# Two transformer-like blocks on one core: a unit's products with the low half of the weights move behind all those with the high half

## The reference, cut to what matters

```python
def first_block(x, mem, ...):
    z = _rmsnorm(x, g_mix) @ w_in                 # 1024 x 11272: three branches, their gates
    kv = _rmsnorm(mem, g_mem) @ w_mem_kv          # cross attention's keys and values
    ...                                           # stick-breaking attention, mLSTM, cross attention
    x = x + (g0 * (y_sb @ w_sb_proj) + g1 * (y_ml @ w_ml_proj) + g2 * (y_x @ w_x_proj)) @ w_out
    x = x + square(relu(_rmsnorm(x, g_mlp) @ w_ff1)) @ w_ff2

def second_block(x, ...):
    proj = rmsnorm(x, norm_mix_pre_w) @ w_in      # dilated attention and a Mamba-2 mixer, their gates
    ...
    h = x + rmsnorm((g_att * att + g_ssm * ssm) @ w_out, norm_mix_post_w)
    f = square(relu(rmsnorm(h, norm_ffn_pre_w) @ w_up)) @ w_down
    return h + rmsnorm(f, norm_ffn_post_w)
```

## Time and profile before

| | |
|---|---|
| median of 3 runs | 1284.5 us |
| the profiled execution's own time | 1283.23 us |
| its span (first to last instruction) | 1281.1 us |
| TensorE matmul (PE) busy | 1234.9 us, 96% |
| TensorE weight load (PEld) busy | 1209.5 us, 94% |
| VectorE (DVE) busy | 799.1 us, 62% |
| ScalarE (ACT) busy | 659.4 us, 51% |
| L236 matmuls | 8976 in 188 units |
| DMA, mean | 164 GB/s |

### The profile page before, as it was taken

The page is one execution under the profiler, slowest core; times in us unless marked ns, Lnnn a source line. Parts: engine busy times, 40 slices in busy tenths (PEclk is TensorE's granted clock), DMA queues, the critical chain, the costliest instruction groups (busy, mean ns, idle before and its releaser), DMA issues. The chain is left out here.

```text
span 1281.1 us, 22409 instructions
## 1 busy us (share of the span) xinstructions
PE 1234.9 (96%) x9900; PEld 1209.5 (94%) x9900; DVE 799.1 (62%) x866; ACT 659.4 (51%) x764; POOL 10.5 (1%) x23
## 2 busy tenths in 40 slices
PE   7999999999999999999989999899899998999996
PEld 6999999999999999999989989898899997999996
DVE  6655666777664557774456567787874554777442
ACT  6443444677543445553344468777864444455330
POOL 0000000000000000000000000000000000000000
PEclk9999999999999999999999999999999998999998
DMA  8553454454665545556545555455356552556540
GB/s 290 165 164 100 136 161 140 141 172 141 198 197 174 188 132 169 193 178 217 189 141 183 157 149 165 148 165 152 128 182 197 186 177 66 171 192 212 183 132 33
DMA packets 210240, 210.27 MB, mean 164 GB/s; under 512 B 6476, under 2 KB 207564, under 8 KB 210144
## 3 DMA queue, kind: packets, MB, share of 16 engines
q1 hardware_dynamic: 207600, 200.30, 49.2%
q0 software_dynamic: 1968, 7.64, 2.1%
q10 hardware_dynamic: 576, 0.90, 0.2%
HBM read 207.73 MB, written 1.09 MB: 163 GB/s over the span
## 5 line engine op out<-in xcount | busy, mean ns | idle before, releaser
L236 PE MATMUL ps<-x_hi,w_hi 128*128 128x256 f32 x2752 | 792.1, 288 | 12.2 <-DVE x_lo L1120 8.7
L236 PE MATMUL ps<-x_lo,w_hi 128*128 128x256 f32 x2752 | 781.5, 284 | 0.0
L236 PE MATMUL ps<-x_hi,w_lo 128*128 128x256 f32 x2752 | 781.3, 284 | 0.0
L204 DVE TENSOR_TENSOR w_lo<-raw,w_hi 128x2048 fp32r<-128x2048 f32 x188 | 429.9, 2290 | 252.1 <-ACT w_hi L198 252.1
L236 PEld LDWEIGHTS ps<-x_hi,w_hi 128*128 128x128 f32 x2752 | 530.8, 193 | 18.7 <-issue 13.6
L236 PEld LDWEIGHTS ps<-x_lo,w_hi 128*128 128x128 f32 x2752 | 531.2, 193 | 0.9
L236 PEld LDWEIGHTS ps<-x_hi,w_lo 128*128 128x128 f32 x2752 | 530.8, 193 | 0.0
L198 ACT CAST w_hi<-raw 128x2048 fp32r<-128x2048 f32 x188 | 355.2, 1899 | 117.6 <-PE ps L236 115.4
L1364 PE MATMUL ps<-arena,cst 128*128 128x256 f32 (+1 forms) x240 | 57.7, 380 | 19.4 <-ACT arena L767 12.2
L236 PE MATMUL ps<-w_hi,x_hi 128*128 128x256 f32 x240 | 69.1, 288 | 2.4 <-DVE w_lo L204 2.4
L1364 PE MATMUL ps<-arena 128*128 128x256 f32 (+3 forms) x448 | 68.3, 341 | 2.3 <-ACT arena L747 2.3
(11 more groups left out here) (174 smaller groups left out, 685.6 us busy)
## 6 DMA issues: line engine op xcount, KB each, us to landing
raw<-in_w_in SPq DMA_DIRECT2D x170, 512.0 KB, 4.7
raw<-in_w_ff SPq DMA_DIRECT2D x64, 512.0 KB, 4.5
raw<-in_w_up SPq DMA_DIRECT2D x32, 512.0 KB, 4.7
raw<-in_w_down SPq DMA_DIRECT2D x32, 512.0 KB, 4.4
raw<-in_w_mem_kv SPq DMA_DIRECT2D x16, 512.0 KB, 5.0
raw<-in_w_out SPq DMA_DIRECT2D x16, 512.0 KB, 4.9
raw<-in_w_ssm_proj SPq DMA_DIRECT2D x16, 512.0 KB, 4.7
raw<-in_w_x_proj SPq DMA_DIRECT2D x8, 512.0 KB, 4.8
```

Of the source, the lines that this page charges most:

```text
L204: nc.vector.tensor_tensor(w_lo[:, s], raw[:, s], w_hi[:, s].bitcast(FP32), ALU.subtract)\
L236: last = nc.tensor.matmul(dst, l, r, start=start and k == 0 and m == 0, stop=stop and k == nk - 1 and m == 2)
```

## The change

In `products` each half unit now makes two loops over `k`: first the products with w_hi (two for each `k`, 16 in all), then the 8 with w_lo. Between the loops stands a wait for w_split. In `begin` the wait for w_split becomes one for w_hi, the semaphore that ScalarE raises. The waits for x's low half (`lo`) stay in the first loop, ahead of both products of their `k`. Unit 0, the helpers and the programs of the other engines stay as they are.

```diff
@@ products
+            def product(k, wt, xt, first, last):
+                if tok:
+                    l, r = xt[:, at + k, o * P:(o + 1) * P], wt[:, s, k, :]
+                else:
+                    l, r = wt[:, s, k, o * P:(o + 1) * P], xt[:, at + k, :]
+                return nc.tensor.matmul(dst, l, r, start=start and first, stop=stop and last)
+
             for k in range(nk):
                 if lo is not None:
                     name, before, per = lo
                     pe.wait_ge(S(name), before + k // per + 1)
-                for m, (wt, xt) in enumerate(((w_hi, x_hi), (w_hi, x_lo), (w_lo, x_hi))):
-                    if tok:
-                        l, r = xt[:, at + k, o * P:(o + 1) * P], wt[:, s, k, :]
-                    else:
-                        l, r = wt[:, s, k, o * P:(o + 1) * P], xt[:, at + k, :]
-                    last = nc.tensor.matmul(dst, l, r, start=start and k == 0 and m == 0,
-                                            stop=stop and k == nk - 1 and m == 2)
+                product(k, w_hi, x_hi, k == 0, False)
+                product(k, w_hi, x_lo, False, False)
+            pe.wait_ge(S(f"w_split{s}"), u // SLOTS + 1)
+            for k in range(nk):
+                last = product(k, w_lo, x_hi, False, k == nk - 1)
             return last
@@ begin
-                pe.wait_ge(S(f"w_split{u % SLOTS}"), u // SLOTS + 1)
+                pe.wait_ge(S(f"w_hi{u % SLOTS}"), u // SLOTS + 1)
```

## The result

In 18 runs each the changed kernel took 1286.46 us in the median (1285.29 to 1288.30), the one before 1283.88 us (1283.00 to 1285.63). The ratio is 1.0020, with a 95% interval of 1.0013 to 1.0028: slower by 2.6 us (1.7 to 3.6), just at what the forecast called the limit of what can be told from no change. The forecast was +0.9 us, with a range of 1283.2 to 1288.4 us. The sign was right; the size was a third of what came.

What follows compares the result with a forecast made beforehand. TensorE's matmuls, busy 96% of the span, were taken to bound the kernel. Costs of 3.3 us in six halves waiting for x_lo, less gains of 2.4, gave +0.9: median 1285.4 us, range 1283.2 to 1288.4.

Steps and rivals of the forecast that it cites:

- The pace and the added waits: All units: the pace stays 0.12 us a product across the new wait, and the 376 added waits cost 0.
- Rival D: The added waits aren't free: at 0.08 us for each of 376, +30 us, 1315 us; chance 0.02.
- The gains, 2.4 us: Earlier starts in gx units 1 and 2, ga unit 2, up unit 2 and up2 unit 2 save 2.4 us in all.
- The 1.9 us at cross unit 1: Cross unit 1 ends 1.9 us earlier, but cross unit 2 still waits for x_lo until 28.06: gain 0.
- rival B: At cross unit 2 x_lo isn't the limit, so 1.9 us more is gained: -1.0, 1283.5 us; chance 0.04.
- E: w_hi comes as late as w_lo, so the gains are missing: +3.3, 1287.8 us; chance 0.04.
- Ga unit 2: Its 1.24 us pause for w_lo goes, with 0.08 us on the product after the restart; it starts without a pause.
- Out, out2, up and cross unit 2: More products behind the last x_lo cost +0.72 in out unit 0, +0.72 in out2, +0.74 in up, +0.3 in cross unit 2.
- the pause in up unit 0: Up unit 0 gets a wait for x_lo that it hadn't, and its half ends 0.7 us later.
- Att and up2 unit 0: Ten products behind the last x_lo cost +0.3 us (bounds 0 and +0.9) and +0.5 us (bounds 0 and +0.8).
- Rival A: Clock falls in new or longer pauses at cross unit 2, out and out2 unit 0: all three +5.2, 1289.7 us; chance 0.12.
- The chances: For the whole kernel's time: same within 0.2% (2.6 us) 0.76, slower 0.20, faster 0.04.

Runs made afterwards that it cites:

- e1_order_only: The two loops in every half, but begin waits for w_split as in the kernel before; 1.0038 of the kernel before, +4.9 us.
- e3_six_halves_only: The kernel before with the two loops only in the six halves that wait for x_lo; 1.0037 of the kernel before, +4.8 us.
- e2_gate_only: The changed kernel with the old order in the six halves that wait for x_lo; 0.9981 of the kernel before, -2.4 us.
- e5_changed_filled: The changed kernel with 23 and 40 idle-filling matmuls in the long pauses before att and up2 unit 0; 1.0020 of the kernel before.
- e8_before_filled: The kernel before with idle-filling matmuls in the long pauses ahead of att and up2 unit 0; 0.9996 of the kernel before.
- e10_pauses_filled: e5_changed_filled with idle-filling matmuls also in the short pauses inside att and up2 unit 0's first halves; 1.0009 of the kernel before.
- e7_two_halves_old: The changed kernel with the old order in the first halves of att and up2 unit 0 alone; 0.9998 of the kernel before.

## Why the prediction was right in sign and too small

- **The pace and the added waits**: right. 0.12 us across the new wait (24.36 to 24.48), and nothing to be seen of 370 of the 376 (e1_order_only against e3_six_halves_only). Rival D is out.
- **The gains, 2.4 us**: right (2.4 by e2_gate_only). The 1.9 us at cross unit 1 turned into a pause in front of cross unit 2, 1.96 us long, as forecast; rival B is out. E, that w_hi isn't early enough, is out too.
- **Ga unit 2**: the forecast's words were wrong, its sum was near. It said that the unit starts and runs without a pause. It did start early (936.12 against 936.65), but paused 0.85 us in its middle. VectorE's w_lo ended at 939.05, 2.5 us later than before, while TensorE had got ahead of that chain. It had waited 1.45 us for the silu before ga unit 0 instead of 2.09, and behind that wait its clock was high, where it had been low before: the stretch from 923 to 929 has 1.00 against 0.84, and from the restart behind the wait to the next helper matmuls (934.16 before, 935.11 now) TensorE gained another 1.6 us. The new order hid its full 16 products there. The forecast had shifted both engines alike, and that the sum came out near it owes something to where the low clock fell.
- **Out, out2, up and cross unit 2**: right to 0.1 us (0.7, 0.7, 0.8, 0.3), and so is the pause in up unit 0 that the trace of before didn't have.
- **Att and up2 unit 0**: the step that failed, as a term that was mis-sized: +0.3 and +0.5 in the forecast, 1.4 and 1.0 in the trace. Its words were "TensorE's clock is low there until about 672.2": the low stretch of the trace of before was taken over as it stood, with only the work behind the last x_lo lengthened. But the change also thins TensorE's work ahead of the last x_lo, from three products a tile to two, and so lengthens its pauses; and in the profiled execution the low clock stays longer, over all ten products behind the last x_lo. E5, e8 and e10 speak for both halves of that, each by one profiled execution: the low stretch went behind the short pauses when only the long one was filled, and went away when the short ones were filled too. Even at the high clock the two halves cost 0.84 each and not 0.3 and 0.5: the forecast had let the ten products make up time by a clock that rises under them, and it didn't rise. From the end of the last x_lo the halves cost 1.14 and 0.88 us, beyond the forecast's own bounds of 0.9 and 0.8.
- **Rival A** had the right mechanism in the wrong places. It looked at the new pauses in front of cross unit 2 and in out and out2 unit 0. In the changed kernel's trace the clock stayed high behind all three. Behind the pause at cross unit 2 it does fall in some executions: the profiles of e2_gate_only, e5_changed_filled and e7_two_halves_old, each with a pause of 1.97 us there, have 0.79 in the stretch where the changed kernel's has 1.00. First e2_gate_only, then the changed kernel:

```profile
26.00:34.00 8.00, 6.04 (x39) 5.86 (x38) 7.34 (x8) 5.42 (x7) 0.00 (x0) 0.79 0.58 197
```

```profile
26.00:34.00 8.00, 6.43 (x51) 6.32 (x52) 5.93 (x8) 4.49 (x5) 0.00 (x0) 1.00 0.54 166
```

  Up to there e5_changed_filled and e10_pauses_filled have the changed kernel's instructions. From the start of cross unit 2 to its second half e5 took 33.56 - 29.13 = 4.4 us, the changed kernel 30.81 - 27.57 = 3.2 and e10 31.26 - 28.00 = 3.3: a fall costs 1.2 us, and of three executions of the same instructions one had it. That fits what the Trainium skill says ("TensorE: Matmul & The Clock Gate", section "What's actually happening"): the gate's timer runs freely. How many of the changed kernel's 18 executions had it isn't known. The profiled one, their shortest, had not, so rival A may hold a part of the 0.5 us that the traces leave open; that is not shown.
- **The chances**: "within 0.2%" had 0.76 and "slower" 0.20; the measured 0.20% lies on the line between them. A net of +0.9 with a mis-sized term of 1.6 us under a limit of 2.6 deserved a larger share for slower. The forecast's own range of -0.9 to +2.8 doesn't come out of the bounds that it names: with those of the two halves and 1.4 us for one fall the ends are -1.3 and +3.2. The +2.6 lies in both.

## What to carry to other kernels

An order that lets work start earlier by putting some of it last must be looked at from both ends: where the early operand was the limit it gains, but where another operand comes in piece by piece it leaves more behind the last piece (here 10 products for 3). The order to look for is the one in which the operand that comes last is used last; taken half by half, it gave -5.6 us where the uniform change gave +2.6. And where TensorE is fed in pieces, its clock belongs into the sum: here eight products that were moved behind the gaps took 1.71 us instead of 0.96.

## What the runs showed of the hardware that wasn't expected

- Forty matmuls back to back didn't secure the clock for the half that followed: with pauses of 1.29 and 0.68 us ahead of groups of products TensorE went at the slow pace from behind them on, and the last eight products took 1.70 us instead of 0.95 (e5_changed_filled, up2 unit 0, one profiled execution). With these pauses filled the granted clock stayed at 1.00 (e10_pauses_filled).
- Behind the same pause of 1.96 or 1.97 us, with the same instructions before and after it, the clock fell in one profiled execution of three, at a price of 1.2 us.
- Filling a pause with idle matmuls paid in the profile where it raised the clock (0.8 and 1.1 us in e8_before_filled's two halves), but hardly in the time of the kernel (0.9996, 0.9987 to 1.0006).
